# Six Strassen groups among the gate and up tiles of a feed-forward block, with GpSimd on its token mixes and lower parts

## The reference, cut to what matters

```python
def swiglu(h, w_gate, w_up, w_down):
    return (jax.nn.silu(h @ w_gate) * (h @ w_up)) @ w_down
...
h = h + swiglu(rms_norm(h, norm_ffn[layer]), w_ff_gate[layer], w_ff_up[layer], w_ff_down[layer])
```

## Time and profile before

| | |
|---|---|
| median of 3 runs | 2019.44 us (2018.93 to 2019.8) |
| the profiled execution, its own time | 2017.43 us |
| its span in the profile | 2015.6 us |
| TensorE busy, share of the span | 97% |
| VectorE, ScalarE, GpSimd busy | 71%, 47%, 4% |

### The profile page before, as it was taken

How to read it: one execution, slowest core, us unless ns; L and a number is a source line. 1 busy time by engine, 2 the same in 40 slices (tenths; PEclk the granted TensorE clock), 3 DMA queues, 4 the chain that set the end, 5 groups by cost and what they waited for, 6 DMA issues and landing times. The chain is left out here.

```text
span 2015.6 us, 29754 instructions
## 1 busy us (share of the span) xinstructions
PE 1950.6 (97%) x11821; PEld 1069.2 (53%) x11821; DVE 1422.2 (71%) x2437; ACT 947.0 (47%) x1628; POOL 71.0 (4%) x51
## 2 busy tenths in 40 slices
PE   9989999999999999999999999999989999999997
PEld 4444444444444884445444854855544444466476
DVE  6979744538667677677478668878866646966777
ACT  4447723324333344347355435445477843634442
POOL 2000000000000102000001000000000000100000
PEclk9999999999999999999999999999989999999999
DMA  7300233324331333322222342435300031424311
GB/s 243 105 1 1 74 85 107 102 59 140 99 102 47 114 118 120 114 74 63 83 69 74 136 127 59 132 114 156 129 1 1 12 104 33 141 65 155 95 63 43
DMA packets 53931, 179.41 MB, mean 89 GB/s; under 512 B 6176, under 2 KB 11936, under 8 KB 53536
## 3 DMA queue, kind: packets, MB, share of 16 engines
q1 hardware_dynamic: 53792, 177.51, 28.4%
HBM read 174.34 MB, written 2.10 MB: 88 GB/s over the span
## 5 line engine op out<-in xcount | busy, mean ns | idle before, releaser
L2192 DVE SCALAR_TENSOR_TENSOR w_lo<-w_raw,w_hi 128x1024 f16<-128x1024 f32 (+3 forms) x359 | 452.6, 1269 | 57.7 <-ACT w_hi L1741 24.4
L1741 ACT ACTIVATE w_hi<-w_raw 128x1024 f16<-128x1024 f32 (+1 forms) x358 | 372.7, 1062 | 201.8 <-DVE w_raw L2212 83.8
L1176 PE MATMUL pS<-xx,w_hi 128*128 128x512 f16 x952 | 361.9, 380 | 1.4 <-DVE xx L2227 1.4
L1178 PE MATMUL pS<-xx,w_lo 128*128 128x512 f16 x952 | 362.2, 380 | 0.0
L1177 PE MATMUL pS<-xx,w_hi 128*128 128x512 f16 x952 | 362.0, 380 | 0.0
L1243 PE MATMUL pS<-arena,w_hi 128*128 128x256 f16 x645 | 175.8, 273 | 0.0
L1244 PE MATMUL pS<-arena,w_lo 128*128 128x256 f16 x645 | 175.8, 273 | 0.0
L1242 PE MATMUL pS<-arena,w_hi 128*128 128x256 f16 x645 | 175.8, 273 | 0.0
L1178 PEld LDWEIGHTS pS<-xx,w_lo 128*128 128x128 f16 x952 | 93.3, 98 | 113.2 <-issue 1.4
L1176 PEld LDWEIGHTS pS<-xx,w_hi 128*128 128x128 f16 x952 | 93.3, 98 | 109.8 <-DVE xx L2227 2.2
L1177 PEld LDWEIGHTS pS<-xx,w_hi 128*128 128x128 f16 x952 | 93.2, 98 | 107.8 <-issue 1.5
(11 more groups left out here) (449 smaller groups left out, 3816.8 us busy)
## 6 DMA issues: line engine op xcount, KB each, us to landing
w_raw<-in_w SPq DMA_DIRECT2D x298, 512.0 KB, 3.7
w_raw<-in_w SPq DMA_DIRECT2D x12, 704.0 KB, 4.2
X<-in_x SPq DMA_DIRECT2D x8, 264.0 KB, 7.2
arena<-in_c SPq DMA_DIRECT2D x2, 1024.0 KB, 6.5
out_t<-X SPq DMA_DIRECT2D x16, 128.0 KB, 1.7
arena<-in_h SPq DMA_DIRECT2D x4, 256.0 KB, 12.5
arena<-in_h SPq DMA_DIRECT2D x2, 512.0 KB, 10.4
w_raw<-in_w SPq DMA_DIRECT2D x2, 384.0 KB, 3.6
```

Source lines behind the costliest of these rows:

```text
L1176: pe.matmul(ps, wh, ah, start=f, stop=False)
L1178: mm = pe.matmul(ps, wl, ah, start=False, stop=l)
L1741: act.activation(to_, from_, ACT.Copy, scale=WS).then_inc(hi_split, 1)
L2192: dve.scalar_tensor_tensor(out=lo_[:, a:], in0=from_[:, a:], scalar=WS, in1=hi_[:, a:], op0=ALU.mult, op1=ALU.subtract).then_inc(lo_split, 1)
```

## The change

Pairs n = 7, 9, 11, 13, 15 and 17 of the 22 become Strassen groups of their own stages (`ffs7`, ...), with the gate tile and the up tile as the two outputs, the two halves of the contraction of 1024 as the blocks inside, and token halves as the blocks of the other operand. The other pairs stay whole tiles (`ffgu` for 0 to 6, `fft8`, `fft10`, ..., `fft18` for 18 to 21).

A group needs the activations `x1` in four mixed forms. ScalarE scales `X` by the norm's gain into `x1g` (8 operations, right after the norm's `norm_copy`), GpSimd mixes four pairs of it (`mix`: one operation of 512 columns and two of 256), ScalarE makes the high parts (`x1t[0]`, in `spread` of n = 1 and 2) and VectorE the lower parts (at n = 2 and 3).

For the hidden tiles GpSimd now runs `mix` and makes both lower parts (`lower`), which VectorE did before. VectorE waits for GpSimd before it writes `src` again: `hidden_ff` waits for `tokens_mixed` and `rhs_ready`. In program order GpSimd does, for each p: `mix`, the weight sum of a later group, `lower` of `src`, `lower` of `sums`. ScalarE makes the high part of `src` at the next even n, after the tanh of that n.

```diff
+GROUPED = (7, 9, 11, 13, 15, 17)
...
+            def mix(b, to):
+
+                pool.tensor_tensor(in_two(to[:, 0:T]), in_two(b[:, HT:3 * HT]), twice(b[:, 3 * HT:4 * HT]), ALU.subtract).then_inc(first_mixed, 1)
+                firsts[0] += 1
+                pool.wait_ge(first_mixed, firsts[0])
+                pool.tensor_tensor(to[:, 2 * HT:3 * HT], b[:, HT:T], to[:, HT:T], ALU.add).then_inc(first_mixed, 1)
+                firsts[0] += 1
+                pool.wait_ge(first_mixed, firsts[0])
+                return pool.tensor_tensor(to[:, 3 * HT:4 * HT], b[:, 0:HT], to[:, 2 * HT:3 * HT], ALU.subtract)
+
+            def lower(r, dst, a, h):
+
+                pool.wait_ge(rhs_hi, r + 1)
+                pool.tensor_tensor(dst, a, h, ALU.subtract).then_inc(rhs_ready, 1)
...
-            add_weights("ffds")
+            for p in range(KD // 2):
+                pool.wait_ge(x1_scaled, 2 * p + 2)
+                mix(x1g[:, p, :], x1m[:, p, :]).then_inc(x1_mixed, 1)
...
+            for p in range(KFF1 // 2):
+                if p == KFF1 // 2 - 2:
+                    add_weights("ffds", 0, 1)
+                pool.wait_ge(computed, PL.s["ff"] + 2 * p + 2)
+                r = PL.r["ff"] + 2 * p
+                if p:
+                    pool.wait_ge(rhs_ready, r)
+                mix(src[:, :, :].rearrange("p a b -> p (a b)"), sums).then_inc(tokens_mixed, 1)
+                while summed_groups < len(GROUPED) and GROUPED[summed_groups] <= 2 * p + 6:
+                    add_weights(f"ffs{GROUPED[summed_groups]}")
+                    summed_groups += 1
+                lower(r, ffh[1][:, p, 0:2 * T], src[:, :, :].rearrange("p a b -> p (a b)"), ffh[0][:, p, 0:2 * T])
+                pool.wait_ge(tokens_mixed, p + 1)
+                lower(r + 1, ffh[1][:, p, 2 * T:4 * T], sums, ffh[0][:, p, 2 * T:4 * T])
+            add_weights("ffds", 1)
...
+            for k in range(KD):
+                act.activation(x1g[:, k // 2, k % 2 * T:k % 2 * T + T], X[:, k, 0:T], ACT.Identity, scale=pcol("g_ffn", k)).then_inc(x1_scaled, 1)
...
+            def spread(n):
+
+                if n in (1, 2):
+                    for p in (2 * n - 2, 2 * n - 1):
+                        act.wait_ge(x1_mixed, p + 1)
+                        act.activation(x1t[0][:, p, :], x1m[:, p, :], ACT.Identity).then_inc(x1_hi, 1)
+                if n > 1:
+                    (sums_hi if n % 2 else hidden_hi)((n - 2) // 2)
...
+            def hidden_ff(n):
+
                 dve.wait_ge(act_out, 17 + n + 1)
                 link(dve.scalar_tensor_tensor(out=tmp[:, 3, :], in0=tmp[:, 1, :], scalar=1.0, in1=tmp[:, 0, :],
                                               op0=ALU.add, op1=ALU.mult))
                 sync()
+                if n > 1:
+                    dve.wait_ge(tokens_mixed, n // 2)
+                    dve.wait_ge(rhs_ready, PL.r["ff"] + n // 2 * 2 - 1)
                 dve.tensor_tensor(src[:, n % 2, :], tmp[:, 3, :], tmp[:, 2, :], ALU.mult).then_inc(computed, 1)
-                if n % 2:
-                    dve.wait_ge(computed, PL.s["ff"] + n + 1)
-                    mix_tokens()
-            pair_lo(KFF1 // 2 - 1, "ff", ffh)
+
+            def grouped(s, n):
+
+                i, o = GROUPED.index(n), s.o0
+                a, b, c, d, e, h = (pS[:, 0, 0:HT], pS[:, 1, 0:HT], pS[:, 2, 0:HT], pS[:, 3, 0:HT], pT[:, 0, 0:HT], pO[:, 0, 0:HT])
+                gate, up = tmp[:, 0, :], tmp[:, 2, :]
+                out_of(s, 0)
+                dve.tensor_tensor(gate[:, 0:HT], a, rs[:, 0:HT], ALU.mult).then_inc(evicted, 1)
+                out_of(s, 1)
+                dve.wait_ge(first_copied, i + 1)
+                dve.tensor_tensor(fy, b, fx, ALU.subtract).then_inc(evicted, 1)
+                dve.wait_ge(evicted, o + 2)
+                dve.tensor_tensor(fz[:, 0:HT], e, fy, ALU.add).then_inc(evicted, 1)
+                out_of(s, 3)
+                dve.tensor_tensor(fz[:, HT:T], fy, d, ALU.subtract).then_inc(evicted, 1)
+                dve.wait_ge(evicted, o + 4)
+                dve.wait_ge(computed, PL.s["ff"] + n)
+                dve.tensor_tensor(in_two(up), in_two(fz), twice(c), ALU.subtract).then_inc(evicted, 1)
+                out_of(s, 5)
+                dve.tensor_tensor(gate[:, HT:T], h, fz[:, HT:T], ALU.subtract).then_inc(evicted, 1)
+                dve.wait_ge(evicted, o + 6)
+                dve.tensor_tensor(gate[:, HT:T], gate[:, HT:T], rs[:, HT:T], ALU.mult).then_inc(gate_scaled, 1)
+                link(dve.tensor_tensor(up, up, rs[:, 0:T], ALU.mult))
```

More of the change, by code:

```diff
@@ L76, with ff_parts @@
 CLOSED = ("ffd7", "up0a", "up1a")
+GROUPED = (7, 9, 11, 13, 15, 17)
+def ff_parts():
+    parts, n = [], 0
+    while n < KFF1:
+        if n in GROUPED:
+            parts.append((f"ffs{n}", "S", n, 1))
+        else:
+            end = min([g for g in GROUPED if g > n] + [KFF1])
+            parts.append((f"fft{n}" if n else "ffgu", "T", n, end - n))
+        n += parts[-1][3]
+    return parts
+FF_PARTS = ff_parts()
+FF_STAGES = [(name, kind, 2 * count, KD, 1) if kind == "T" else (name, kind, 1, KD // 2, 1) for name, kind, _, count in FF_PARTS]
+SIX += tuple(name for name, kind, n, _ in FF_PARTS if kind == "T" and n)
 UP_A = 16
@@ L1082, in _, with add_weights @@
             norm_power("x0", meta=True)
-            def add_weights(name):
+            def add_weights(name, first=0, end=None):
                 s = S[name]
-                for g in range(s.n):
+                for g in range(first, s.n if end is None else end):
                     raw, _, _ = PL.sums[PL.unit[s.factor(g, 2, 0)]]
@@ L1259, in down @@
                 else:
-                    product(parts[1], 0, 0, ops, copies, 0, n // 2 - 1)
+                    product(parts[1], 0, 0, by_blocks(ops), copies, 0, n // 2 - 1)
                 for k in range(n - 2, n):
@@ L1268, in down @@
                             pe.wait_ge(rhs_ready, r + n)
-                        product(parts[1], g, x, ops, copies, n // 2 - 1 if m is not None and g == 0 and x == 0 else 0, n // 2)
+                        product(parts[1], g, x, by_blocks(ops), copies, n // 2 - 1 if m is not None and g == 0 and x == 0 else 0, n // 2)
                 if m is not None:
@@ L1606, in _ @@
             lead(S["ffgu"], "x1", "ffgu")
-            for j in range(LEAD + 2, 2 * KFF1):
-                out_T(S["ffgu"], j, xr)
-            down([S["ffd0"], S["ffds"], S["ffd7"]], ffh, PL.r["ff"], 0, "x2")
+            for name, kind, n0, _ in FF_PARTS:
+                s = S[name]
+                if kind == "T":
+                    for j in range(0 if n0 else LEAD + 2, s.n):
+                        out_T(s, j, xr)
+                    continue
+                pe.wait_ge(x1_lo, KD // 2)
+                for x in range(len(PRODUCTS)):
+                    product(s, 0, x, x1_block, GROUPED.index(n0), 0, s.k)
+            down([S["ffd0"], S["ffds"], S["ffd7"]], ffh, PL.r["ff"], len(GROUPED), "x2")
             lead(S["cv"], "xb", "cv")
@@ L2740, in _ @@
             norm("x1")
-            mixed = [0]
+            mixed = [KFF1 // 2]
             def mix_tokens():
@@ L2838, in _ @@
             parts = [S["ffd0"], S["ffds"], S["ffd7"]]
-            down(parts, "x2", 0, 0.5 / WS, True, True)
+            down(parts, "x2", len(GROUPED), 0.5 / WS, True, True)
             s, i = S["ffd7"], HALVED.index("x2") + 1
```

112 lines of the change are left out of this document (86 added, 26 removed).

## The result

The changed kernel takes 2034.48 us (median of 4 runs, 2031.62 to 2037.16), the kernel before 2019.53 in the same comparison: a ratio of 1.0078, with a 95% interval of 1.0066 to 1.009 (the comparison's own figure, not the quotient of the two medians, which is 1.0074). It is slower by 15 us. The forecast was 2041, range 2016 to 2066. The profiled execution took 2034.45 us, 17.0 more than that of before (2017.43), and its span is 17.1 longer.

What follows compares the result with a forecast made beforehand. The prediction took the kernel's stage to be bound by TensorE, and after the change by VectorE and GpSimd excluding each other. The profiled 2017.43 us plus 21.9 gives 2039.3, with 2.0 for the median 2041 us; range 2016 to 2066.

Steps and rivals of the forecast that it cites:

- the exclusion of the two engines: VectorE operations with two SBUF operands and GpSimd sums exclude each other for full length: 20.4 us against TensorE's 19.4.
- The sum: First group at 500.5, five rounds of 23.2, pair 18 at 626.5 instead of 604.77: 21.9 us added.
- A round: From one group's hidden tile to the next group's: 23.2 us, 3.8 over TensorE's 19.4.
- The plain part: Round's first part, VectorE waiting to write src while GpSimd mixes, sums weights, makes the first lower part: 9.1 us.
- The group part: Rest of a round on VectorE: splits, sums, taking out, rescaling, hidden tile, with GpSimd's second lower part: 14.1 us.
- Lower parts: GpSimd's 1024-column operation with float16 operand and result: taken as 2.35 us, bounds 1.18 and 3.5.
- The start: Before the first group, both engines' 52.9 us of work delays pair 6's gate read; TensorE waits 9.7 us.
- The last group: From pair 17's group at 616.5 to pair 18, which needs bank 0 at c (the group's hidden tile) + 11.3 = 626.5.
- TensorE's waits: About 3 us before each further group, at bank 0; the group's results come early, so TensorE adds nothing more.
- TensorE stayed the bound: Rival: GpSimd's work hides beside VectorE's, rounds of 19.9 us at most, gain mostly stays: 2012 us; chance 0.18.
- Only the start costs: Rival: rounds fit nearly, only the 9.7 us wait before the first group remains: 2017 to 2026 us; chance 0.12.
- GpSimd is slower still: Rival: lower parts over 3.5 us or lost turns, +4 us a round: 2057 to 2072 us; chance 0.12.

Runs made afterwards that it cites:

- D: Changed kernel plus one GpSimd sum of 1024 columns in spare space for p = 3 to 7, which nobody waits for: 2043.08 us, 1.0124.
- E: Changed kernel plus two GpSimd fills of 1024 columns, which read nothing, for p = 3 to 7: 2035.0 us, 1.009.
- A: Changed kernel with VectorE again mixing the hidden tiles and making their lower parts, six groups kept: 2030.43 us, 1.006.
- H: Changed kernel without GpSimd's four mixes for x1, groups taking unmixed operands (part of the computation left out): 2031.55 us, 1.0071.
- G: Changed kernel with four groups, at pairs 11, 13, 17 and 19, in place of six, scratch tiles moved: 2012.62 us, 0.9975.
- C: Changed kernel with a second src, so VectorE's write waits for the lower part of the pair before: 2031.34 us, 1.0067.

## Why the prediction was right, and by how much it was out

**Direction and mechanism.** Right: the exclusion of the two engines bounds the rounds, at the place named (the gate tile of the plain pair) and at a second one, and pair 18 starts late. D shows that a further reading operation on GpSimd costs most of its length (1.7 of 2.34 us) though nobody waits for it, E that fills cost nothing, A that VectorE's own work with the mixes and lower parts back on it gives 21.5.

**The sum.** Pair 18 starts at 621.87, 17.10 us after 604.77, and the span is 17.1 longer: nothing behind the stage absorbs or adds time, as forecast. The forecast shift was 21.9. The 4.8 between are three terms, all too high: first group at 498.33 in place of 500.5 (2.2); from there to the last group 114.37 in place of 116 (1.6); from the last group to pair 18 9.17 in place of 10.2 (1.0). The other 1.7 us between 2041 and 2034.48 lie in rounding (0.3) and in the step from the profiled execution to the median: 2.0 in the kernel before, nothing here (2034.45).

**Signs named beforehand.** Seen: groups 23 us apart, GpSimd busy 9.7 us of each round, longer VectorE instructions beside GpSimd's. Missed in size: the first wait, 7.29 and not 8 to 10; the wait before each further group, 1.44 and not about 3; the first lower part, 2.13 and not 2.35 or longer; pair 18 at 621.87 and not about 627.

**A round.** Right as a whole (22.94 against 23.2) with errors of both signs inside. The plain part, from 542.49 to 550.71, is 8.2 us, not 9.1: the two splits and the hidden operation that VectorE gets in were charged 1.8 us of GpSimd's time, and the extra length of GpSimd's three mix operations (1.65 + 1.06 + 1.13 against 1.27 + 0.73 + 0.73) is 1.1, since one of them began before GpSimd did. The first lower part takes 2.13, not 2.35. The group part is 14.7, not 14.1 (550.71 to 565.4).

**Lower parts.** These were the unknown operation, bounded at 1.18 and 3.5. In the groups of GpSimd by shape in the changed kernel:

```profile
L1139 POOL TENSOR_TENSOR arena<-sq,arena 128x1024 f16<-128x1024 f32 x11 | 28.1, 2550 | 28.1 <-ACT arena L1879 28.1
L1139 POOL TENSOR_TENSOR arena<-src,arena 128x1024 f16<-128x1024 f32 x11 | 24.2, 2197 | 3.1 <-ACT arena L1879 3.1
```

2.20 and 2.55 with the waits for a turn, 4.7 for the two, which is the forecast's number, but not its meaning: the forecast took 2.35 each undisturbed, and undisturbed it is 2.12 to 2.13. The nearest row of before was 10% too high, and the waits for a turn make up the difference.

**The start.** The size was somewhat too high (a wait of 7.29 against 9.7), and the reason given holds only in part. The forecast added both engines' work to 52.9 us "if no moment is lost". H shows that this sum does not set the wait: taking 10.7 us out of it took 3.1 out of the wait. A takes GpSimd's mixes and lower parts of the hidden tiles out of it, 14.8 us by the forecast, gives VectorE the same work at its lower price, and the wait is 7.80. Each engine goes by its own program order and stands idle in between, VectorE 8.8 us in three waits (4.02, 2.64, 2.12). The forecast named only the scalings, and took them to lie inside the sum; the wait of VectorE's weight sum on GpSimd's it did not see. That lost moments and over-counted turns nearly cancelled is luck. What sets the wait is not shown.

**The last group.** 9.17 us to pair 18, with no wait inside it, as no later group's weights are summed there. The forecast used the 11.3 us of a full round from c.

**TensorE's waits.** The forecast had some 3 us at one place in each round. They are two, 1.44 and 1.56, and the second (the seventh product's weights, split late) the forecast had ruled out: "TensorE adds nothing to the round". With the 0.16 by which a record of a matmul outlasts the distance between starts, they are 3.3 of the 3.5 us that a round lacks.

**The rivals.** TensorE stayed the bound in none of the rounds. "Only the start costs" is out too: rounds of 22.94 cost 2.2 each over before. "GpSimd is slower still" is out with 4.7 for two lower parts. One reading of the forecast is wrong without consequence: 489.90 to 604.80 is 0.9 us more than eleven pairs, not less.

**Where the gain went.** Six groups save 7.8 us of TensorE's starts. Its ten waits in the stage sum to 19.9 us (7.29, 0.64, and four times 1.44 and 1.56); with 0.16 for each, and 2.4 for the slower clock in the first round (22.60 long, less 0.8 for its wait, less 19.4), they are 23.9 of the 24.9 that 17.1 and 7.8 make. Some 0.7 of the last 1.0 is a term of the forecast: it gave a group 9.06 us of TensorE (0.108 a matmul), though it had read 0.109 from the earlier trace rows. Where TensorE does not wait, a group takes 9.17 (612.70 to 621.87, 84 matmuls). So a group saves 1.19 us and not 1.29, six save 7.1, and a round needs 19.5. The rest stays unexplained. Four groups with plain pairs between keep their gain (G).

## What to carry to other kernels

Before work is moved from VectorE to GpSimd, add up what both do with SBUF operands, GpSimd's reading operations at full length. If the sum is over the time of the stage, and GpSimd needs longer for the work than VectorE did (7.0 against 3.8 us here), expect the move to make the stage longer (22.9 against 21.5 us a round here), whatever the idle shares on the page say. A denser form for TensorE keeps its saving where the other engines keep up: follow each dense stretch by a loose one and leave the start of a stage alone (four groups gained 5 us where six lost 15).

## What the runs showed of the hardware

**GpSimd with a float16 result.** 1024 columns float32 less float16 to float16 take 2.12 to 2.13 us undisturbed, a sum of 1024 columns in float32 2.34 to 2.35.

**Which operations exclude each other.** A fill on GpSimd beside a VectorE split costs neither engine time: two fills take 1.96 us, the split 1.21 (E). GpSimd operations and VectorE's with two SBUF operands alternate when both have work (C); each change of turn lengthened the later one by 0.3 to 0.5 us in the mixes.

**The clock.** The forecast expected that each stand of TensorE would be followed by a stretch at 1.2 GHz. In the changed kernel's later rounds, with stands of 1.44 and 1.56, the granted clock stays 1.00. In C, whose waits before a group alternate between about 2.35 and 0.68, it falls behind the longer ones and not behind the shorter. Length alone does not decide it: the stand of the earlier trace rows, followed by 0.57, is 1.42 us long,

```profile
1633.84 0.39 PE L1176 MATMUL pS<-xx,w_hi 128*128 128x512 f16 x1 [1.42 <-DVE xx L2227]
```

and TensorE was busy for only 0.58 of the 2 us from 1632, while between the stands of the changed kernel's rounds it is busy throughout. Windows of 2 us in C, behind a stand of 2.35 that ended at 542.33:

```profile
542.30:544.30 2.00, 1.97 (x12) 1.52 (x13) 2.00 (x3) 2.00 (x3) 1.84 (x3) 0.61 0.77 207
544.30:546.30 2.00, 2.00 (x12) 1.43 (x11) 1.97 (x3) 1.59 (x4) 2.00 (x2) 0.53 1.02 407
546.30:548.30 2.00, 2.00 (x21) 1.79 (x19) 2.00 (x2) 2.00 (x4) 2.00 (x2) 1.00 0.15 50
```
